# Rotary swap of dimensions: product with a permutation matrix against transfers inside SBUF

## What is computed

```python
x1, x2 = xr[..., :8], xr[..., 8:16]
xr = xr * cos + concatenate([-x2, x1], axis=-1) * sin      # dimensions 16 to 63 stay as they are
```

## Time and profile before

| | |
|---|---|
| Runs shown | 1155.46 us median of 3 (1154.97 to 1156.65) |
| The profiled execution | 1161.27 us; its span, from the first to the last instruction, 1159.4 us |
| Mean granted TensorE clock | 0.984 of full speed |
| Busy: TensorE, its weight loads, VectorE, ScalarE, GpSimd | 1118.0 (96%), 1055.6 (91%), 816.5 (70%), 526.2 (45%), 12.0 us (1%) |
| Chain that ended last, by engine | PE 73%, DVE 17%, ACT 6%, issue 2%, DMA 2% |
| Costliest lines of that chain | PE mm L422 62%, DVE lo L1117 5%, DVE cacc L1197 4%, ACT hi L799 3% |
| DMA | 228.61 MB, mean 197 GB/s |

### The profile page before, as it was taken

How to read it: one execution, slowest core, us unless ns; L and a number is a source line. 1 busy time by engine, 2 the same in 40 slices (tenths; PEclk the granted TensorE clock), 3 DMA queues, 4 the chain that set the end, 5 groups by cost and what they waited for, 6 DMA issues and landing times.

```text
span 1159.4 us, 19626 instructions
## 1 busy us (share of the span) xinstructions
PE 1118.0 (96%) x8440; PEld 1055.6 (91%) x8440; DVE 816.5 (70%) x1090; ACT 526.2 (45%) x605; POOL 12.0 (1%) x26
## 2 busy tenths in 40 slices
PE   6999888999999899999999999999999999999998
PEld 5878677999999798988999999999899899999998
DVE  5865576776766599885787788768989377666442
ACT  4544444656333543553653444345355455444432
POOL 4000000000000000000000000000000000000000
PEclk9999889999999999999998999999999999999998
DMA  7533323878887164424778998965443275676540
GB/s 211 182 121 135 108 79 105 326 267 297 315 285 252 38 218 153 138 74 158 259 257 288 319 313 294 326 213 168 166 146 110 82 261 183 204 252 202 179 165 37
DMA packets 131494, 228.61 MB, mean 197 GB/s; under 512 B 5925, under 2 KB 59539, under 8 KB 131409
## 3 DMA queue, kind: packets, MB, share of 16 engines
q1 hardware_dynamic: 130404, 227.11, 58.1%
q0 software_dynamic: 672, 0.06, 0.1%
q10 hardware_dynamic: 333, 0.21, 0.1%
HBM read 226.30 MB, written 1.05 MB: 196 GB/s over the span
## 4 chain that ended last, share of the span: by engine, by line
PE 73%; DVE 17%; ACT 6%; issue 2%; DMA 2%; SPq 0%; DVEq 0%; ACTq 0%
PE mm L422 62%; DVE lo L1117 5%; DVE cacc L1197 4%; ACT hi L799 3%; PE mm L461 2%; PE pv L479 2%; DMA raw<-in_w_out_dram 1%; PE pa L506 1%; DVE ada_acc L1138 1%; DVE sB L1205 1%; PE pv L521 1%; PE pa L501 1%; PE pv L706 1%; DMA raw<-in_w_ffn_in_dram 1%; DVE pB L1496 1%
## 5 line engine op out<-in xcount | busy, mean ns | idle before, releaser
L422 PE MATMUL mm<-act_hi,hi 128*128 128x256 f32 x1760 | 493.0, 284 | 6.0 <-ACT act_hi L861 2.7
L422 PE MATMUL mm<-act_hi,lo 128*128 128x256 f32 x1760 | 486.6, 280 | 0.0
L1117 DVE TENSOR_TENSOR lo<-raw,hi 128x2048 fp32r<-128x2048 f32 (+1 forms) x160 | 361.9, 2265 | 173.6 <-ACT hi L799 172.2
L422 PE MATMUL mm<-act_lo,hi 128*128 128x256 f32 x1760 | 470.1, 280 | 0.0
L799 ACT ACTIVATE hi<-raw 128x2048 fp32r<-128x2048 f32 (+1 forms) x160 | 301.5, 1889 | 226.7 <-PE mm L422 180.5
L422 PEld LDWEIGHTS mm<-act_hi,hi 128*128 128x128 f32 x1760 | 332.5, 189 | 11.8 <-issue 9.5
L422 PEld LDWEIGHTS mm<-act_hi,lo 128*128 128x128 f32 x1760 | 332.9, 189 | 0.8 <-issue 0.7
L422 PEld LDWEIGHTS mm<-act_lo,hi 128*128 128x128 f32 x1760 | 322.4, 189 | 0.0
L422 PE MATMUL mm<-u_hi,hi 128*128 128x256 f32 x608 | 170.7, 281 | 0.0
L422 PE MATMUL mm<-u_lo,hi 128*128 128x256 f32 x608 | 170.4, 280 | 0.0
L422 PE MATMUL mm<-u_hi,lo 128*128 128x256 f32 x608 | 169.2, 278 | 0.0
(11 more groups left out here) (247 smaller groups left out, 995.1 us busy)
## 6 DMA issues: line engine op xcount, KB each, us to landing
ada_raw<-in_ada_w_dram SPq DMA_DIRECT2D x96, 512.0 KB, 6.0
raw<-in_w_ffn_in_dram SPq DMA_DIRECT2D x88, 512.0 KB, 6.0
raw<-in_w_in_dram SPq DMA_DIRECT2D x40, 1024.0 KB, 5.1
raw<-in_w_ffn_out_dram SPq DMA_DIRECT2D x20, 1024.0 KB, 6.0
raw<-in_w_up_dram SPq DMA_DIRECT2D x16, 1024.0 KB, 6.6
raw<-in_w_down_dram SPq DMA_DIRECT2D x16, 1024.0 KB, 7.8
raw<-in_w_out_dram SPq DMA_DIRECT2D x12, 1024.0 KB, 5.1
raw<-in_w_in_dram SPq DMA_DIRECT2D x16, 512.0 KB, 5.3
```

What stands on the lines that cost most here:

```text
L422: ins = pe.matmul(o, w[:, kk, fs], a[:, k, :], start=(k == 0 and i == 0 and f % 2 == 0), stop=(ends and i == len(pairs) - 1), skip_group_c ...
L1117: v(dve.tensor_tensor(lo[:, c % RING, 0:nk, :], raw[:, c % RING, 0:nk, :], hi[:, c % RING, 0:nk, :].bitcast(F32), ALU.subtract), "lo_done")
```

## The change

The rotation product and its matrix go. In their place ScalarE, after each evacuation of queries or keys, issues four DMAs that copy eight partitions each (for two heads, the upper eight dimensions to the lower eight and back) from `qk` to a new buffer `turned` of the same shape, inside SBUF. Before them it waits for its own evacuation and for two semaphores. The sign is in the frequencies: those of a head's first eight dimensions are negative, so their sine is, and the cosine stays. VectorE waits for the four transfers (`turned_landed`, 64) and multiplies `turned` with the sine table, where it read the bank before. The dimensions that aren't rotated have a sine of 0; GpSimd clears `turned1` at the start, and `turned2` after each of two ("down", 1) groups, whose buffers share its memory.

TensorE's order changes with it. First block: ("in",1), ("in",2) chunk 0, lambdas, gate product, then scores of unit 0. Layers: ("in",1), both chunks of ("in",2), scores of unit 0. The scores of unit 0 wait for three of four rotated parts instead of four; unit 4 waits for the fourth.

```diff
-C_ID, C_ROT, C_ONE = 0, P, 2 * P
-C_ADD, C_MUL, C_FREQ = 3 * P, 6 * P, 9 * P
+C_ID, C_ONE = 0, P
+C_ADD, C_MUL, C_FREQ = 2 * P, 5 * P, 8 * P
...
-        if d < half:
-            c[p + half, C_ROT + p] = -1.0
-        elif d < 2 * half:
-            c[p - half, C_ROT + p] = 1.0
         if d < 2 * half:
-            c[p, C_FREQ] = freq[d % half]
+            c[p, C_FREQ] = freq[d % half] * (-1.0 if d < half else 1.0)
...
+        turned1 = sb("turned1", [P, KD, S], on=mixA)
...
+        turned2 = sb("turned2", [P, KD, S], on=mixB)
...
@@ TensorE
-            def rope(qk, names="qk"):
-
-                for name in names:
-                    for j in range(2):
-                        i = 2 * j
-                        k = (0 if name == "q" else 4) + 2 * j
-                        full(pe.matmul(bank(i)[:], rot, qk[:, k:k + 2, :], start=True, stop=True), i)
...
+                if u == 4:
+                    pe.wait_ge(sem("rope_done"), n.seen("rope_done"))
...
             chunk(("in", 1), 0, act_hi, act_lo)
-            pe.wait_ge(sem(freed(("in", 0))[0]), freed(("in", 0))[1])
-            rope(qk1, "q")
             chunk(("in", 1), 1, act_hi, act_lo)
-            pe.wait_ge(sem(freed(("in", 1))[0]), freed(("in", 1))[1])
-            rope(qk1, "k")
             chunk(("in", 2), 0, act_hi, act_lo, token_major=True)
             wait("lam_ready")
             full(pe.matmul(bank(2)[:, 0:LAYERS], ones[0:1, :], lams[0:1, 8:8 + LAYERS], start=True, stop=True), 2)
-            wait("rope_done", 4)
-            scores(qk1, 0)
-
             pe.wait_ge(sem("gate_weights_loaded"), 64)
             b = bank(2)
             for k in range(KD):
                 ins = pe.matmul(b[0:F0 + MH, 0:S], wg[:, k, :], hng[:, k, :], start=(k == 0), stop=(k == KD - 1))
             full(ins, 2)
+            wait("rope_done", 3)
+            scores(qk1, 0)
+            n("rope_done", 1)
...
-                chunk((l, "in", 1), 0, act_hi, act_lo)
-                pe.wait_ge(sem(freed((l, "in", 0))[0]), freed((l, "in", 0))[1])
-                rope(qk2, "q")
-                chunk((l, "in", 1), 1, act_hi, act_lo)
-                chunk((l, "in", 2), 0, act_hi, act_lo, token_major=True)
-                pe.wait_ge(sem(freed((l, "in", 1))[0]), freed((l, "in", 1))[1])
-                rope(qk2, "k")
-                chunk((l, "in", 2), 1, act_hi, act_lo, token_major=True)
-                wait("rope_done", 4)
+                product((l, "in", 1), act_hi, act_lo)
+                for j in range(2):
+                    chunk((l, "in", 2), j, act_hi, act_lo, token_major=True)
+                wait("rope_done", 3)
                 scores(qk2, 0)
+                n("rope_done", 1)
@@ ScalarE
+            def turn_dims(qk, turned, blk, g):
+
+                a.settle()
+                act.wait_ge(sem("rope_done"), 4 * blk)
+                act.wait_ge(sem("turned_cleared"), blk + 1)
+                half = QK // 8
+                k = slice(4 * g, 4 * g + 4)
+                for h in range(2):
+                    for dst, src in ((QK * h, QK * h + half), (QK * h + half, QK * h)):
+                        act.dma_start(turned[dst:dst + half, k, :], qk[src:src + half, k, :]).then_inc(sem(f"turned_landed{g}"), 16)
...
             evacuate(("in", 0), qk1[:, 0:4, :])
+            turn_dims(qk1, turned1, 0, 0)
...
             evacuate(("in", 1), qk1[:, 4:8, :])
+            turn_dims(qk1, turned1, 0, 1)
...
                     evacuate((l, "in", g), qk2[:, 4 * g:4 * g + 4, :])
+                    turn_dims(qk2, turned2, 1 + l, g)
@@ GpSimd
+            pool.memset(turned1[:, :, :], 0.0).then_inc(sem("turned_cleared"), 1)
             p(pool.memset(wg[:, :, :], 0.0))
...
+            for name in (("down", 1), (0, "down", 1)):
+                pool.wait_ge(sem("mm_done"), groups[name][1][-1] + 1)
+                pool.memset(turned2[:, :, :], 0.0).then_inc(sem("turned_cleared"), 1)
@@ VectorE
-            def rope(qk, blk, names="qk"):
+            def rope(qk, turned, blk, names):
+                wait(f"turned_landed{'qk'.index(names)}", 64)
                 for j in [j for j in range(4) if "qqkk"[j] in names]:
-                    i = 2 * (j % 2)
-                    b = full(i)
...
-                    v(dve.tensor_tensor(z, b[:].rearrange("p (a s) -> p a s", a=2), sn, ALU.mult), f"bank{i}_free")
+                    v(dve.tensor_tensor(z, turned[:, k, :], sn, ALU.mult))
```

More of the change, by code:

```diff
@@ L61 @@
 BEFORE_PI = 3.1415925
-C_ID, C_ROT, C_ONE = 0, P, 2 * P
-C_ADD, C_MUL, C_FREQ = 3 * P, 6 * P, 9 * P
-C_ALL = 9 * P + 1
+C_ID, C_ONE = 0, P
+C_ADD, C_MUL, C_FREQ = 2 * P, 5 * P, 8 * P
+C_ALL = 8 * P + 1
 def constants():
@@ L286, in two_blocks @@
         posf = sb("posf", [1, 2 * S], on=start)
+        lamr = sb("lamr", [1, LAYERS * 2, 2, QK], on=start)
+        lamp = sb("lamp", [1, LAYERS * 2, QK], on=start)
         start.close()
@@ L293, in two_blocks @@
         hmA = sb("hmA", [P, 2, S], on=mixA)
-        lamr = sb("lamr", [1, LAYERS * 2, 2, QK], on=mixA)
-        lamp = sb("lamp", [1, LAYERS * 2, QK], on=mixA)
         lams = sb("lams", [1, 16], on=mixA)
+        turned1 = sb("turned1", [P, KD, S], on=mixA)
         mixA.close()
@@ L319, in two_blocks @@
         ident = cst[:, C_ID:C_ID + P]
-        rot = cst[:, C_ROT:C_ROT + P]
         ones = cst[:, C_ONE:C_ONE + P]
@@ L1284, in _ @@
             wait("tables_ready")
-            rope(qk1, 0, "q")
+            rope(qk1, turned1, 0, "q")
             advance(groups[("in", 1)][1][1])
-            rope(qk1, 0, "k")
+            rope(qk1, turned1, 0, "k")
             advance(groups[("in", 2)][1][0])
@@ L1475, in _ @@
                     if i in (5, 7):
-                        rope(qk2, 1, "q" if i == 5 else "k")
+                        rope(qk2, turned2, 1, "q" if i == 5 else "k")
                     advance(c)
```

## The result

The changed kernel took 1163.2 us (median of 5 runs, 1161.94 to 1167.08) against 1154.97 us for the kernel before on the same chip (5 runs, 1154.02 to 1156.65): ratio 1.0086, 95% interval 1.0067 to 1.0105. The forecast was 1158.7 us, range 1153.0 to 1163.0. The sign was right, the size was not, and the time lies just outside the range.

The account below looks back on a forecast made before the run. TensorE was busy 96% of the span, but VectorE was taken to set the pace around the rotations. Terms 0.8 + 1.8 + 0 + 0.8 - 0.2 = +3.2 us on 1161.27, less 5.8 to the median: 1158.7 us, range 1153.0 to 1163.0.

Parts of the forecast that it names:

- Bank 2: First block: gate product waits for VectorE's copy of lambda until about 59.4 us, scores behind it; 0.8 us lost.
- The clock: First block: after TensorE's 5.6 us pause the gate product runs at the low clock; +1.8 us, ends 0 and 3.6.
- Landing: First block: the keys' transfers land in 2.2 us, within the 2.5 us before VectorE needs them; 0 us.
- ScalarE's issues: Layers: waits and four issues delay ScalarE's next split, 1.6 us a group; +0.4 us a layer, 0.8 in all.
- Issues of no length: Layers: if issues took no time, both VectorE waits would be gained, 1.8 us in all; sum +0.6 instead of +3.2.
- Keys' product in the layers: Layers: removing TensorE's second 1.72 us gains nothing, since VectorE leads there after 443.80.
- VectorE's source: VectorE's sine product, reading SBUF instead of a bank, keeps its 0.68 us; 0 us.
- Constants: Kernel start: the constants are 64 KB shorter ahead of x; -0.2 us, at most 0.3.
- From execution to median: Whole kernel: the runs' median lies 5.8 us below the profiled execution, a difference carried over to the forecast.
- Faster: Rival, first block: bank 2 doesn't hold the gate product, ("in",2) 1 starts 4.8 us earlier; -4.2, 1151.3 us; chance 0.12.
- Late landing: Rival, first block: the keys' transfers share DMA engines with a load, taking 5.1 us; +2.6, 1161.3 us; chance 0.18.
- Hardly a change: Rival: the clock doesn't fall and issues are short; 0.8 - 0.2, nothing from the layers, 1156.1 us; chance 0.25.

Follow-up runs that it names:

- scores first: Changed kernel with the first scores put back ahead of the gate product, lambda's product left late: 1159.26 us, ratio 1.0044 to the kernel before.
- two other kernels with that wait: Change kept in the first block only (1157.57 us, ratio 1.0027); changed kernel with all 24 transfers issued by GpSimd (1156.56 us, ratio 1.0014).
- first comparison: The changed kernel against the kernel before on the same chip: 1163.2 us against 1154.97, ratio 1.0086.
- second comparison: The unaltered changed kernel measured again against the kernel before: 1161.12 us against 1155.21, ratio 1.0064.
- lambda early: Changed kernel with lambda's product moved ahead of ("in",1) 1 and its copy ahead of the keys' rotation: 1154.09 us, ratio 0.9991; again 1154.55, 0.9992.
- layers only: The change made in the two layers alone, the first block keeping its product and old order: 1157.24 us, ratio 1.0022 to the kernel before.

## Why the prediction was wrong

- *Bank 2*: right. Forecast: gate product near 59.45, 0.8 us lost. Measured: 59.89, held by L1290; the scores stood behind it as forecast.
- *The clock*: right. Forecast 1.8 us, measured 5.25 - 3.62 = 1.63; but 1.9 us with the scores first (5.50 us) and 2.5 us in two other kernels with that wait (6.14 and 6.07 us), inside the end of 3.6. That 1.8 came out so near is in part luck: it was the price of another pause, before another chunk.
- *Landing*: nearly. 2.33 us to landing against 2.2; the issues were longer, and VectorE waited 0.34 us where I had 0. Chunk ("in",2) 1 was forecast near 65.7 and came at 65.98.
- ***ScalarE's issues***: **the step that failed.** I took 0.35 us for each, from small loads at the start, hence 1.6 us a group, VectorE 1.33 us late and +0.4 us per layer. An issue took 0.63 us at the least, the pause between evacuation and split was 3.10 us, VectorE waited 2.80, and a layer lost 1.6 to 1.7 us. The mechanism was right (the wait at 443.80 went, the cover of 0.27 us was all there was); the term was four times too small. My upper bound, from the 0.59 us of the first issue, was 1.4 a layer; of two prices far apart I had taken the one with the larger count, though no row was a transfer of this kind. Twice the 1.2 us missing turn +3.2 into +5.7; the trace has +6.1. With +5.7 the forecast would have been 1161.2 us, inside its range; the other 2 us of the first comparison's +8.2 stay open, and the second comparison (+5.9) doesn't have them.
- *Issues of no length* would have given +0.6. The trace says otherwise: four issues took 2.6 to 3.0 us on ScalarE, and the landing behind the last of them 2.33 us. The Trainium skill, DMA: Bandwidth & Descriptors, "Issuing engines are not separate DMA queues", calls the time to initiate a DMA usually small beside the DMA; this trace does not agree. What such issues would have given, both waits of the earlier trace rows (0.97 and 0.82 us), came only where nothing stands behind them: with GpSimd issuing, the layers gained 1.3 and 0.9 us.
- *Keys' product in the layers, VectorE's source, GpSimd's clears*: right. L1219 took 0.69 us from SBUF as it had 0.68 from its bank; a clear took 1.80 us and nobody waited for it.
- *Constants*: forecast -0.2 us; VectorE's `parT<-pv` row came 0.14 us earlier. The start moved by up to 1.4 us in the other kernels, so this one number shows little.
- *From execution to median*: I carried the 5.8 us over by which the profiled execution stood above the runs. The sum against the median was thus the sum of the terms, which is sound; the two profiled spans however differ by 1.8 us only (1159.4 and 1161.2), because untouched stretches were slower in the profile of before: from layer 0's first maximum to layer 1's `act_hi` 324.6 us against 322.7, for one. A reader of the two spans alone would have seen under a third of the 6.1 us.
- *The rivals.* "Faster" was wrong for this kernel, but its mechanism was a good one: with bank 2 free the value chunk came 5.3 us earlier (I had 4.8). "Late landing" came to 0.34 us, far from its 2.6. "Hardly a change" fell with both of its conditions.

## What to carry to other kernels

When work leaves the busiest engine, ask which buffer its next instruction needs, and where in another engine's queue the instruction stands that gives it back: one matmul and a copy moved ahead brought the next chunk 8 us forward here, while the 9.8 us of TensorE's busy time removed had gained nothing by themselves. DMA issues are instructions of the engine that issues them; put them in a queue with nothing behind, and price them from a row of the same kind of transfer or at the upper bound. For a change of 0.5% compare stretches between two fixed rows, not spans, and let the first row stand behind the kernel's start, which moved by up to 1.7 us between these kernels.

## What the hardware showed unexpectedly

- A transfer inside SBUF (8 partitions, 32 KB) took 0.63 us of ScalarE's queue (the first of a group up to 0.75) and 0.52 of GpSimd's, the same for half the bytes; small loads at the start had taken down to 0.28.
- The same 16 matmuls took 3.62 us when TensorE had been busy, 3.61 after pauses of 0.5 (lambda early) and 1.29 us (layers only), and 5.25, 5.36, 6.14 and 6.07 us after pauses of 6.14, 6.22, 6.54 and 6.76 us, with a granted clock of 0.50 in the us in which the first of them started. With the scores first it was 5.50 us after 3.62 us, four small matmuls and 1.66 us more of pause before them.
